# Hybrid decoder step: other work for TensorE beside HGRN preparation, chunks and sample states

## What is computed

```
ada = silu(c) @ w_ada + b_ada          # shift1 scale1 gate1 shift2 scale2 gate2, per sequence
h = rms(x) * g * (1 + scale1) + shift1
q, f, i, g, u = split(h @ w_in)        # five projections of 512 columns
# HGRN2 (4 heads of 128): f' = lb + (1-lb) sigmoid(f);  k = 1 - f';  v = i
#   state = exp(cum_last) * state + (k exp(last - cum))^T v      per chunk
#   o = masked(q k^T decay) v + (q exp(cum)) state
o_h = rms(o) * gain * silu(g)
# S5: complex diagonal recurrence over u, y = gelu(...)
y = y * sigmoid(y @ w_glu + b_glu);  o_s = rms(y) * gain
x = x + gate1 * ([o_h | o_s] @ w_out)
x = x + gate2 * moe(adaLN(x))          # 32 experts, top 2 of the best of 4 groups
y = rms(x) * gain * (1 + scale_f) + shift_f   # scale_f, shift_f = silu(c) @ w_ada_final
```

## Time and profile before

| | us |
|---|---|
| median of 3 runs (924.2 to 928.5) | 925.13 |
| the profiled execution, its own time | 927.4 |
| its span | 925.7 |
| TensorE busy | 700.2 (76%) |
| VectorE busy | 344.1 (37%) |
| ScalarE busy | 208.4 (23%) |
| POOL busy | 87.8 (9%) |

### The profile page before, as it was taken

How to read it: one execution, slowest core, us unless ns; L and a number is a source line. 1 busy time by engine, 2 the same in 40 slices (tenths; PEclk the granted TensorE clock), 3 DMA queues, 4 the chain that set the end, 5 groups by cost and what they waited for, 6 DMA issues and landing times.

```text
span 925.7 us, 8257 instructions
## 1 busy us (share of the span) xinstructions
PE 700.2 (76%) x2974; PEld 375.9 (41%) x2974; DVE 344.1 (37%) x874; ACT 208.4 (23%) x445; POOL 87.8 (9%) x134
## 2 busy tenths in 40 slices
PE   3799999989969976775799996088759678788700
PEld 1377787744434436653554432033223223233200
DVE  2494836466524343354135526001001101101267
ACT  5311233335244441100111112011001101101131
POOL 1001011201010000000100000411001010100140
PEclk9899999999989985676899997579779889989955
DMA  9682020247450202003962068549998999999362
GB/s 340 215 320 91 1 91 1 92 182 277 155 121 1 91 13 78 1 11 94 380 233 82 24 280 317 76 144 376 372 414 345 406 406 389 402 408 409 147 204 102
DMA packets 50042, 187.22 MB, mean 202 GB/s; under 512 B 12475, under 2 KB 17723, under 8 KB 34134
## 3 DMA queue, kind: packets, MB, share of 16 engines
q1 hardware_dynamic: 32678, 155.39, 43.5%
q10 hardware_dynamic: 10320, 16.10, 5.5%
q0 software_dynamic: 7008, 15.25, 5.4%
HBM read 176.84 MB, written 17.22 MB: 210 GB/s over the span
## 4 chain that ended last, share of the span: by engine, by line
PE 56%; DMA 18%; DVE 10%; ACT 6%; issue 5%; SPq 2%; ACTq 1%; POOL 1%; POOLq 0%; DVEq 0%
PE ps L1539 53%; DMA sb<-in_moe_w_up 13%; DVE sb L930 6%; DMA sb<-in_w_ada 3%; ACT sb L710 2%; PE ps L1588 2%; SPq L349 1%; DMA token_of_row<-sb 1%; POOL token_of_row L531 1%; DVE sb L1520 1%; DVE sb L1532 1%; DMA sb<-y_rows,sb 1%; DMA out_hgrn_sample<-sb 1%; ACTq L793 1%; DMA sb<-h_rows,sb 0%
## 5 line engine op out<-in xcount | busy, mean ns | idle before, releaser
L1539 PE MATMUL ps<-sb 128*64 128x512 f32 (+9 forms) x2590 | 647.1, 509 | 99.9 <-DMA sb<-in_moe_w_up 51.2
L1539 PEld LDWEIGHTS ps<-sb 128*128 128x128 f32 (+4 forms) x2590 | 327.7, 170 | 386.8 <-issue 317.5
L930 DVE TENSOR_TENSOR sb<-sb 128x16 f32<-128x16 f32 (+18 forms) x368 | 162.5, 482 | 100.1 <-ACT sb L710 46.3
L930 DVE TENSOR_TENSOR sb<-ps,sb 128x256 f32<-128x256 f32 (+6 forms) x65 | 26.2, 425 | 222.7 <-ACT sb L876 188.9
L1588 PE MATMUL ps<-sb 128*128 128x128 f32 (+1 forms) x208 | 31.2, 298 | 38.6 <-DMA sb<-h_rows,sb 34.7
L1588 PEld LDWEIGHTS ps<-sb 128*128 128x128 f32 (+1 forms) x208 | 27.0, 196 | 55.4 <-DMA sb<-h_rows,sb 34.8
L876 ACT ACTIVATE sb<-ps 128x256 f32<-128x256 f32 x16 | 6.2, 385 | 177.6 <-PE ps L1539 177.6
L539 POOL DMA_INDIRECT sb<-h_rows,sb x16 | 16.3, 1020 | 157.9 <-PE ps L1588 155.5
L1506 DVE COPY sb<-ps 128x512 f32<-128x512 f32 x16 | 11.1, 692 | 45.7 <-PE ps L1539 45.7
L710 ACT COPY sb<-ps 32x144 f32<-32x144 f32 x64 | 26.3, 411 | 7.4 <-PE ps L1539 5.9
L656 ACT ACTIVATE sb<-ps 128x288 f32<-128x288 f32 x12 | 4.9, 411 | 90.4 <-PE ps L1539 90.4
(11 more groups left out here) (230 smaller groups left out, 358.3 us busy)
## 6 DMA issues: line engine op xcount, KB each, us to landing
sb<-in_moe_w_gate SPq DMA_DIRECT2D x32, 1024.0 KB, 13.5
sb<-in_moe_w_up SPq DMA_DIRECT2D x32, 1024.0 KB, 15.9
sb<-in_moe_w_down SPq DMA_DIRECT2D x32, 1024.0 KB, 8.5
sb<-in_w_ada SPq DMA_DIRECT2D x12, 2048.0 KB, 8.1
sb<-in_w_in SPq DMA_DIRECT2D x5, 2048.0 KB, 10.3
sb<-in_w_ada_final SPq DMA_DIRECT2D x4, 2048.0 KB, 11.6
sb<-in_w_out SPq DMA_DIRECT2D x2, 2048.0 KB, 7.8
sb<-in_x_prompt SPq DMA_DIRECT2D x4, 512.0 KB, 9.9
```

Source lines behind the costliest of these rows:

```text
L930: return dve.tensor_tensor(out, x0, x1, op)
L1539: return pe.matmul(out, lhsT, rhs, start=start, stop=stop, skip_group_check=True)
```

## The change

Semaphores `identity`, `cmask` and `before` are folded into counts of `const`, and buffers are placed anew (the S5 gate's sigmoids, `sT` and `Vm` in slot 3, `QhM` in the conditioning rows' space, `g1b` and `B2b` in slot 2). The order of the pieces and their slots becomes an explicit list; slot 3 is left out from the value weights on:

```diff
+            (WI, 0, "proj_mm", 17), (GLU, 1, "glu_mm", SF), (WG, 2, "proj_mm", 22),
+            (G_3[0], 0, "ada_mm", 17), (G_3[1], 1, "ada_mm", 18), (G_3[2], 0, "ada_mm", 19), (G_3[3], 1, "ada_mm", 20),
+            (w_o[0], 0, "wo_mm", TILES), (w_o[1], 1, "wo_mm", TILES)]
```

Each entry holds the piece, its slot, and the count at which the slot is free again. SP now also issues what ScalarE issued (the sample states, the gate rows, x, the norm's rows, the state stores and the late loads):

```diff
+                if n == N_S0[0]:
+                    sp.wait_ge(S["s5_fintr"], 2)
+                    sp.wait_ge(S["s5_X"], SF)
+                    load_s0(1)
+                if n == N_S0[1]:
+                    sp.wait_ge(S["kh_tr"], H)
+                    load_s0(0)
+            sp.wait_ge(S["proj_mm"], 22)
+            sp.wait_ge(S["ada_stored"], 128)
+            token_rows(sp, 2, g1b, S["bc_g1"])
+            sp.wait_ge(S["o_mm"], PT)
+            sp.wait_ge(S["vm_ready"], 1)
+            for t in range(TILES):
+                if t == PT:
+                    sp.wait_ge(S["mix_s5"], 1)
...
+                if t == 0:
+                    token_rows(sp, 4, A2b, S["bc_h2"])
+                    sp.dma_start(gffn, a["norm_ffn"].to_broadcast([P, D])).then_inc(S["bc_h2"], 16)
+                    token_rows(sp, 3, B2b, S["bc_h2"])
```

The state stores, the late loads, expert pieces 3, 4, 5, then 0, 1 (all output tiles done) and 2 with gate2's rows (all tiles normalised) follow there. The conditioning goes to four strips of one bank:

```diff
-                            q = 32 * ((2 * g + a_) % 4)
-                            ins = mm(banks[h][q:q + C9, :], cT[:, c, :], w[:, k, D * a_ + 512 * h:D * a_ + 512 * h + 512], c == 0, False)
+                            q = 32 * (2 * a_ + h)
+                            ins = mm(bank[q:q + C9, :], cT[:, c, :], w[:, k, D * a_ + 512 * h:D * a_ + 512 * h + 512], c == 0, False)
```

TensorE's HGRN preparation has the value projection (units 12 to 16, into banks 0, 1, 6, 7, 0) and the S5 gate's units, and no gate projection:

```diff
+            proj_rows(12)
+            proj_rows(13)
+            pe.wait_ge(S["s5_finout"], 2)
+            turn_keys(0)
+            proj_rows(14)
+            proj_rows(15)
+            turn_keys(1)
+            proj_rows(16)
+            glu_unit(0)
+            turn_keys(2)
+            for m in range(1, SF):
+                glu_unit(m)
+            turn_keys(3)
```

ScalarE evacuates in that order, each before it copies the head's keys (`proj_rows(12 + 2 * h)` and the next for h < 2; `proj_rows(16)` and `glu_gate(0)` for head 2; `glu_gate(1)` to `(3)` for head 3). In the chunks, one unit of the gate projection (into bank 0) stands between a tile's two chunks, and the final conditioning (into bank 1) beside it:

```diff
+            GATE = {2: (0, 0, KC), 4: (0, 0, 3, 6, KC)}[CPT]
+            scores(0)
+            w_now[0] = next_piece()
+            for t in range(PT):
+                for j in range(CPT):
+                    chunk_update(CPT * t + j)
+                    if j == 0:
+                        intra(t)
+                        if t == 1:
+                            pe.wait_ge(S["glu_rt"], 1)
+                        if t >= 1:
+                            ada_part(3, (0, 1, 3)[t - 1], ps[1])
+                    elif GATE[j] < GATE[j + 1]:
+                        gate_rows(t, GATE[j], GATE[j + 1])
+                    if j == CPT - 1 and t >= 1:
+                        turn_mix(t - 1)
+                    chunk_out(CPT * t + j)
+                if t == 0:
+                    glu_squares()
+                if t == 2:
+                    ada_part(3, 2, ps[1])
+                scores(t + 1)
+            gate_rows(PT, 0, KC)
+            turn_mix(PT - 1)
+            intra(PT)
+            state_out(0)
+            state_out(1)
...
+            state_update(0, 0)
+            state_update(0, 1)
...
+            out_part(0, 0)
+            state_update(0, 2)
+            state_update(0, 3)
+            pe.wait_ge(S["ada_out"], 20)
+            out_part(0, 1).then_inc(S["wo_mm"], 1)
+            state_update(1, 0)
+            state_update(1, 1)
+            pe.wait_ge(S["sc_mask"], TILES)
+            out_part(1, 0)
+            state_update(1, 2)
+            state_update(1, 3)
+            turn_mix(PT)
+            out_part(1, 1).then_inc(S["wo_mm"], 1)
```

VectorE's order in the loop, with the S5 gate's parts (they lay behind the samples before):

```diff
             mask(0)
+            glu_gated()
             for t in range(PT):
...
+                    if j == 0 and t >= 1:
+                        norm_o(t - 1)
+                mask(t + 1)
+                out_gate(t)
+                if t == 0:
+                    glu_norm()
+                if t == 1:
+                    glu_scale()
+            norm_o(PT - 1)
+            out_gate(PT)
+            norm_o(PT)
```

More of the change, by code:

```diff
@@ L202, in decoder_step @@
         Qt = v2(MIXT + 4 * NT, H, NT)
-        sT = [v2(HT + 2304 + 512 * k, H, P) for k in range(2)]
-        QhM = v3(HT + 3328, H, 4, NS)
+        HG = 3 * SLOT
+        sT = [v2(HG + 512 * k, H, P) for k in range(2)]
+        QhM = v3(ROWS8, H, NB, 4 * TS)
         KhT = v2(EXT, TILES, DH)
@@ L276, in decoder_step @@
         SMALL = 3
+        CONST = {"sums": 1, "identity": 2, "masks": 3, "scan": 4, "before": 5}
         def u_offset(r, q, s):
@@ new lines, in _ @@
+            sp.wait_ge(S["s_upd"], NCH)
+            sp.dma_start(o["hgrn_prompt"][0, 0].rearrange("h k v -> k h v"), Sr[NCH % 3]).then_inc(S["hs_out"], 16)
+            for half in range(2):
+                sp.wait_ge(S["s0_new"], half + 1)
+                sp.dma_start(o["hgrn_sample"][0, 4 * half:4 * half + 4].rearrange("b h k v -> k (b h) v"),
+                             S0[half].rearrange("k b h v -> k (b h) v")).then_inc(S["s0_out"], 16)
+            sp.wait_ge(S["us_mm"], 2 * H)
+            expert_piece(0, 3)
@@ L611, in _, with ada_rows @@
             act.activation(par[7], par[8], ACT.Sin).then_inc(S["prm_exp"], 1)
-            def ada_rows(g, banks):
+            def ada_rows(g, bank):
                 act.wait_ge(S["ada_mm"], (6, 12, 16, 20)[g])
                 for h in range(2):
-                    for v in (2 * g, 2 * g + 1):
+                    for a_ in range(2):
+                        v, q = 2 * g + a_, 32 * (2 * a_ + h)
                         r = 32 * (v % 4)
-                        act.copy(rows8[r:r + C9, v // 4, h * 512:(h + 1) * 512], banks[h][r:r + C9, :]).then_inc(S["ada_out"], 1)
+                        act.copy(rows8[r:r + C9, v // 4, h * 512:(h + 1) * 512], bank[q:q + C9, :]).then_inc(S["ada_out"], 1)
             def ada_col(v):
@@ L742, in _ @@
                 act.activation(d1, d1, ACT.Exp, scale=-1.0).then_inc(S["e_ready"], 1)
-                for unit in (12, 13, 14) if h < 3 else (12,):
-                    proj_rows(unit + 3 * h)
+                if h < 2:
+                    proj_rows(12 + 2 * h)
+                    proj_rows(13 + 2 * h)
+                elif h == 2:
+                    proj_rows(16)
+                    glu_gate(0)
+                else:
+                    for m in range(1, SF):
+                        glu_gate(m)
                 act.wait_ge(S["kh_tr"], h + 1)
@@ L1556, in _, with ada_part @@
             pe.wait_ge(S["ada_out"], 1)
-            def ada_part(g, j, banks):
+            def ada_part(g, j, bank):
                 w = next_piece().rearrange("p c n -> p (c n)").rearrange("p (c n) -> p c n", c=KS)
@@ L1569, in ada_part @@
                         for a_ in range(2):
[L1570 to L1571 removed]
+                            q, row = 32 * (2 * a_ + h), 4 * g + 2 * a_ + h
+                            ins = mm(bank[q:q + C9, :], ident[0:16, row:row + 1].to_broadcast([16, C9]), bias16, False, True)
                 ins.then_inc(S["ada_mm"], 1)
@@ L1746, in scores, with intra @@
                 ins.then_inc(S["sc_mm"], 1)
-            scores(0)
-            pe.wait_ge(S["proj_act"], 22)
-            pe.wait_ge(S["proj_dve"], TILES)
-            for t in range(TILES):
+            def intra(t):
                 r = ROWS[t]
@@ new lines, in state_update @@
+            def state_update(half, h):
+                done = NCH + 3 * half
+                rows = slice(32 * half, 32 * half + 32)
+                if half == 0 and h == 0:
+                    pe.wait_ge(S["vm_ready"], 2)
+                if h == 0:
+                    pe.wait_ge(S["s_upd"], done)
+                if half == 1 and h < 2:
+                    pe.wait_ge(S["s0_new"], 1)
+                if h >= 2:
+                    pe.wait_ge(S["s_upd"], done + h - 1)
+                mm(ps[6 + h % 2][:, :], KhT[rows, PT, P * h:P * (h + 1)], Vm[rows, :, P * h:P * (h + 1)], True, True)\
+                    .then_inc(S["us_mm"], 1)
@@ L1842, in out_proj @@
                     pe.wait_ge(S["wo_t"], t - 1)
-                for j in range(2):
-                    ins = out_part(t, j, range(H if t < 2 else 0, KC))
-                ins.then_inc(S["wo_mm"], 1)
+                out_part(t, 0)
+                out_part(t, 1).then_inc(S["wo_mm"], 1)
             def router_logits(out, t0, t1):
```

457 lines of the change are left out of this document (221 added, 236 removed).

## The result

The changed kernel took **881.37 us** (median of 4 runs, 877.77 to 883.40) against 926.51 us (924.2 to 928.5) of the kernel before on the same chip: ratio 0.951, 95% interval 0.9465 to 0.9553, 45 us faster. The forecast was 895.2.

What follows compares the result with a forecast made beforehand. DMA bounds the expert stage from 646 us, so gains come from TensorE's gaps ahead of it: 15 + 8.4 + 6.7, rounded to 30, off 927.4 gives 897.4, or 895.2 against the median; range 882 to 911.

Steps and rivals of the forecast that it cites:

- The frame: Whole kernel: the expert stage only shifts, and large matmuls fill TensorE's gaps ahead of it; 30 us gained.
- two stay the most, and I price the edit at nothing: Conditioning matmuls: four column strips in one bank still cost 0.216 us a pass, as two strips did.
- rival 1: Conditioning: four strips run at once, a pass falls to 0.108 us, kernel 887 us (885 to the median); chance 0.12.
- B: From the first scores to the first output tile: 142.1 us instead of 150.5, a gain of 8.4.
- Part A: From S5's end at 258.3 to the first scores: these start near 330.0 instead of 344.89, gain 15 us.
- The 4.7 for the third tile: Part B, third tile: TensorE waits 4.7 us because S5 scaling precedes the state update in VectorE's queue.
- Rival 4: Warm small groups fall to 0.9 us, first units of each burst to 6.95; 10 less, 885 us; chance 0.15.
- rival 2: Chunk loop: VectorE and ScalarE set its time, each of four tiles losing 3 to 4 us more; 909 us; chance 0.18.
- rival 3: Part A: sample states' load holds up issue of the four stores, head 0 is 7 us later; 902 us; chance 0.1.
- rival 5: Chunk loop's clock stays at its old level, 75 us on top of 895, 970 us; chance 0.04.
- rival 6: The fills do nothing, each gap only moves; just part C is gained, 918 us; chance 0.02.
- Part C: Behind the first output tile: router logits gain 4.7 us and ranks 2.0, together 6.7.
- D: From the end of the ranks to the first gathered tile turned; forecast gain 0.

Runs made afterwards that it cites:

- both marks: The changed kernel run again unchanged, in the first and third jobs, for comparison with the runs beside it: 881.53 and 877.55 us.
- the filler: Changed kernel with six throw-away full matmuls in TensorE's wait before the ranks: 876.45 us, ratio 0.941.
- The late pieces: Changed kernel with two of the six pieces of the first experts issued as late as in the kernel before: 884.56 us, ratio 0.950.

## Why the prediction was right and wrong

**The frame held.** The expert stage only shifted (320.8 and 319.8 us), the fills mostly fit into their waits, and no wait for the new order of SP's queue or for POOL's copies shows in the loop.

**The step that failed first: "two stay the most, and I price the edit at nothing".** Four strips do run together, as rival 1 had it: 32 passes take 3.1 us in four strips and 6.5 in two. In B the conditioning took 7.6 us and its bias 1.0, instead of 15.6 together: 7 us of the miss. The row in front of me was two strips at 0.216; it shows that two overlap when two are in use and says nothing of a limit. In the start stage the same saving (2.88 against 5.42 us for 24 passes) was worth nothing, since the u projection then waited 3.93 us for its weights and began at 50.34 instead of 50.41.

**S5 was assumed to stand still.** Part A began at 258.3 by assumption. Beside S5 the conditioning was cover: half as long, it leaves waits of 3 us, the clock falls, and the two Y blocks run at half speed. This is the same step again: the edit that I priced at nothing. The Trainium skill, "TensorE: Matmul & The Clock Gate", section "HAM oscillation — how this bites in real kernels", describes loops in which each burst starts cold behind a wait for a DMA; the windows agree on the cold start, here behind a wait for VectorE (0.53 behind 3.04 us of idle). I looked for a rule against this change only at the place where I priced it at nothing. Behind S5, part A was right to about 1 us: with S5 on time (257.3) the first scores stood at 329.90, forecast 330.0, and the issue took 7.17, forecast 7.07. In the changed kernel, with S5 late, the issue takes 1.88 and gives 5.2 us back, so the net loss was 3.8, not 8.6.

**Part B, 142.1 forecast and 123.7 measured.** Beside the strips (7.0):
- The state products: 6.8 us instead of 11.8. The price was a row of before at 0.184 a pass; at the full clock it is 0.106. I had scaled the small groups to a warm loop and left this one at the old clock. 5.0 us.
- The waits: 5.6 instead of 9.4. The 4.7 for the third tile did not appear. The output of a chunk waits for the update of the chunk before, which VectorE had done ahead of the S5 scaling; I had it wait for its own. The last gate unit and the last mixed tile waited 2.30 and 2.53, forecast 1.5 and 1.9. Together 3.8.
- State updates 7.9 instead of 8.8; the units with 512 columns 64.2 instead of 62.6; small groups 27.7, forecast 27.0. The rest, some 4 us, is how busy rows overlap at their ends: the shapes sum to 122.3, the timeline has 118.1 busy.

Rival 4 (a warm loop) was right on the clock and wrong on its price: the small groups took 1.11 us each at a clock of 1.00 (27.7 for 25), where it had 0.9 and I had 1.08 from a row at 0.78. Rivals 2, 3, 5 and 6 fell.

**Part C, 6.7 forecast and 2.8 measured.** Router logits and ranks moved up as told, but with the conditioning parts ahead of them gone they ran slower: the ranks at a clock of 0.50, 4.99 us instead of 3.3, and the router at 0.82, 8.45 instead of 7.0. The router's part changes with the execution (7.03 in both marks). Of the 1.7 us of the ranks the filler gave 0.9 back, with the clock at 0.62; that the rest is the clock too is not shown. Some 0.8 us of C's miss stays unexplained.

**D was not a step at all: 8.0 us.** The prediction had "the expert stage only shifts" begin at the ranks. Between lie POOL's read of the flag and its scattered writes. Before, the one ran against the expert pieces and the other against the loads of conditioning rows that follow them; SP now issues the last pieces 20.9 us ahead of the ranks' end instead of 3.2. The late pieces give 7 of the 8 back. Another part may be ScalarE: before, it copied the last conditioning rows (567.01 to 569.4, behind a wait of 4.16 for TensorE) ahead of the routing's exponent, and the first weights waited 3.51 us for it. That was only read in the trace of before, not tried.

**The range.** Its low end, 882, was made from each case by itself. Strips (10 us) and warm loop (10 us) don't exclude each other: together they are 875 by my own prices, and two independent terms on one side belong into one far end. Yet this is not what happened. The strips came; the warm loop's 10 us did not, for the small groups took 27.7 us and the first two bursts of part A 14.96 and 14.93, as forecast. What carried the time past the low end beside the strips were terms of no rival: D with 8.0, the state products with 5.0, overlap with 4 and waits with 3.8, against 3.8 lost by S5 and 3.9 in C. That misses of both signs left it only 0.6 us outside the range is luck.

## What to carry to other kernels

A matmul that nobody waits for may still be worth its time: before shortening it, look what TensorE does in the gap, and price the neighbours at the lower clock. Price every term of a loop at one level of the clock, the one that the new loop will have, and add independent surprises on the same side when drawing the range. When transfers move earlier, follow them to what stands behind them in the same queue, and to the small DMAs that both used to run beside, and expect a gain there too.

## What the runs showed of the hardware

- Matmuls with 9 columns of weights and 512 moving take 0.43 us a pass and strip; one, two and four strips gave 13.4, 6.5 and 3.1 us for 32 passes (each up to the start of the load behind them), whatever the bank and, within eight matmuls, the order.
- Work added to TensorE made S5 end 9.7 us earlier (1.0 of it from ahead of the added work); the clock over its Y blocks went from 0.53 to 1.00. Without it, the clock stayed at the lower level through 11.5 us without a gap, behind a wait of 3.05.
- Four small stores issued from ScalarE's queue took 1.88 us or 7.17, with the last of POOL's stores issued 15 or only 7 us earlier, and SP's last 2 MB of weights 22 or 14; which of the two counts is open.
- Beside streaming weights a flag's read by POOL took 3.4 to 3.8 us. Beside loads of conditioning rows the landing of the last scattered write took 6.2 to 6.8 us, instead of 2.3 at a DMA share of 0.06.
- The small groups of the chunk loop (eight passes of 128 columns) took 1.08 us in a row at a clock of 0.78 and 1.11 on average at 1.00.
- In the kernel before, and in the same with four strips, the chunk loop ran its second tile at a clock of 0.58 and of 0.93. Why the same matmuls get one level in one execution and the other in the next is open.
